# Three experts fixed ahead of the routing, the third one's weights in the out product's buffers, and a sorted tile turned early

## What is computed

```python
scores = jax.nn.sigmoid((h @ router_w).astype(jnp.float32))
sel = scores + router_b.astype(jnp.float32)
grouped = sel.reshape(T, N_EXPERT_GROUPS, EXPERTS_PER_GROUP)
gscore = lax.top_k(grouped, TOP_K)[0].sum(-1)
g = jnp.argmax(gscore, axis=-1)
in_group = jnp.take_along_axis(grouped, g[:, None, None], axis=1)[:, 0]
_, loc = lax.top_k(in_group, TOP_K)
expert = g[:, None] * EXPERTS_PER_GROUP + loc
...
hg = jnp.einsum('td,edf->tef', h, w_gate)
hu = jnp.einsum('td,edf->tef', h, w_up)
act = jax.nn.silu(hg) * hu * gates[..., None].astype(h.dtype)
return jnp.einsum('tef,efd->td', act, w_down)
```

## Time and profile before

| | us |
|---|---|
| median of three runs | 548.09 (547.16 to 549.73) |
| span of the profiled execution | 544.1 |
| TensorE busy (matmul) | 480.4, 88% |
| VectorE busy | 236.0, 43% |
| ScalarE busy | 148.2, 27% |
| GpSimd busy | 104.4, 19% |
| moved by DMA | 164.64 MB, mean 303 GB/s |

### The profile page before, as it was taken

The page is one execution under the profiler, slowest core; times in us unless marked ns, Lnnn a source line. Parts: engine busy times, 40 slices in busy tenths (PEclk is TensorE's granted clock), DMA queues, the critical chain, the costliest instruction groups (busy, mean ns, idle before and its releaser), DMA issues. The chain is left out here.

```text
span 544.1 us, 8978 instructions
## 1 busy us (share of the span) xinstructions
PE 480.4 (88%) x3278; PEld 233.3 (43%) x3279; DVE 236.0 (43%) x590; ACT 148.2 (27%) x289; POOL 104.4 (19%) x187
## 2 busy tenths in 40 slices
PE   2788979899969999995996999899998999999893
PEld 1135669655559644573344333333333333333331
DVE  2698994999963300867663101111011101111045
ACT  3645794532147610151102010110001100101142
POOL 3000250988870203500500000000000000000300
PEclk9988999999999999995998999999999999999998
DMA  8993046449497999220696999999999999999932
GB/s 278 339 400 112 1 154 217 166 166 363 143 391 269 369 366 417 82 86 1 239 385 243 410 423 418 418 418 416 421 421 419 419 417 419 417 420 421 403 120 116
DMA packets 42571, 164.64 MB, mean 303 GB/s; under 512 B 3314, under 2 KB 4106, under 8 KB 32676
## 3 DMA queue, kind: packets, MB, share of 16 engines
q1 hardware_dynamic: 35440, 144.22, 67.3%
q10 hardware_dynamic: 4580, 11.91, 5.8%
q0 software_dynamic: 2512, 7.99, 4.0%
HBM read 152.77 MB, written 11.34 MB: 302 GB/s over the span
## 5 line engine op out<-in xcount | busy, mean ns | idle before, releaser
L754 PE MATMUL psum<-arena 128*64 128x512 f32 x672 | 150.7, 601 | 16.7 <-DVE arena L1656 7.8
L754 PEld LDWEIGHTS psum<-arena 128*64 128x64 f32 x672 | 49.8, 138 | 103.7 <-issue 101.9
L767 PE MATMUL psum<-arena 128*64 128x512 f32 x336 | 75.9, 592 | 0.0
L1661 DVE TENSOR_TENSOR arena<-arena,psum 128x256 f32<-128x256 f32 x21 | 8.8, 421 | 143.4 <-ACT arena L1110 143.2
L1916 POOL DMA_INDIRECT arena<-sorted_outputs,src_u x6 | 5.7, 951 | 244.1 <-DMA sorted_outputs<-arena 242.6
L767 PEld LDWEIGHTS psum<-arena 128*64 128x64 f32 x336 | 25.7, 137 | 45.9 <-issue 45.9
L1110 ACT ACTIVATE arena<-psum 128x256 f32<-128x256 f32 x21 | 8.0, 383 | 130.0 <-PE psum L754 114.5
L664 PE MATMUL psum<-arena 128*128 128x512 f32 x96 | 42.2, 594 | 0.0
L1125 ACT ACTIVATE arena<-psum 128x512 f32<-128x512 f32 x19 | 11.3, 597 | 58.0 <-PE psum L767 58.0
L664 PEld LDWEIGHTS psum<-arena 128*128 128x128 f32 x96 | 17.9, 190 | 21.2 <-issue 20.9
L1656 DVE COPY arena<-arena 128x512 f32 x31 | 13.1, 423 | 30.4 <-issue 30.4
(11 more groups left out here) (355 smaller groups left out, 657.3 us busy)
## 6 DMA issues: line engine op xcount, KB each, us to landing
arena<-in_w_gate SPq DMA_DIRECT2D x32, 1024.0 KB, 15.7
arena<-in_w_up SPq DMA_DIRECT2D x32, 1024.0 KB, 18.1
arena<-in_w_down SPq DMA_DIRECT2D x16, 2048.0 KB, 15.2
arena<-in_w_mod SPq DMA_DIRECT2D x12, 2048.0 KB, 13.0
arena<-in_w_in SPq DMA_DIRECT2D x3, 2048.0 KB, 19.2
sorted_outputs<-arena ACTq DMA_DIRECT2D x38, 128.0 KB, 6.3
arena<-in_w_out SPq DMA_DIRECT2D x2, 2048.0 KB, 16.7
arena<-modulation_rows ACTq DMA_DIRECT2D x4, 1024.0 KB, 10.7
```

Of the source, the lines that this page charges most:

```text
L754: last = mm(bank[0][HALF * t:HALF * t + HALF, :], xs[:, side, k, :], gu[:, :, k, t * 256:t * 256 + 256], start=(k == 0), stop=(k == KD - 1))
L767: last = mm(bank[4][HALF * h:HALF * h + HALF, :], hiddenT[:, s * P + t * HALF:s * P + t * HALF + HALF], dn[:, 2 * t + s, h * 512:h * 512 + ...
```

## The change

Experts 0, 4 and 8 (`EARLY`) now stand at places 0, 1 and 2 whatever the counts. Set 2 has gate and up in slots 7 and 8 and down in slot 6, and the third's gate and up are issued as soon as the out product has ended. The sorted tiles move to slot 6 (tiles 0 to 3; tile 3 lies over the routing tiles, tile 4 over the picked first rows), and tile 5 takes tile 0's place, once that has been turned. TensorE turns tile 0 right behind the second gate product of expert 0, ahead of its down product. SP asks for the fourth's gate and up ahead of the third's down. When expert 0 has at most 128 rows, its unneeded passes are counted in `gated` before tile 0 is turned. The second key has changed: by rank, the turn is rank + 1.75 up to rank 9 and half the rank from rank 10, which puts the smallest experts between the largest.

```diff
+EARLY = (0, 4, 8)
...
-        hsr = view(slot(7), 6, D)
+        hsr = [view(at, D) for at in (slot(6), slot(6) + 1024, slot(6) + 2048, slot(6) + 3072, F + 12544, slot(6))]
...
-            b = (3, 0, 6)[j]
-            return view(slot(b), 2, KD, DE), view(slot(b + 2), 4, D)
+            gu, dn = ((3, 5), (0, 2), (7, 6))[j]
+            return view(slot(gu), 2, KD, DE), view(slot(dn), 4, D)
...
-            load_down(1, 1)
+            load_down(1, EARLY[1])
+            sp.wait_ge(S("wo_ready"), 6)
+            load_gate_up(2, EARLY[2])
+
+            def load_sorted(t):
+                sp.dma_start(hsr[t], hsd[t * P:(t + 1) * P, :]).then_inc(S(f"hs_in{t}"), 16)
+
             sp.wait_ge(S("tok_sent"), 16 * 6)
-            for t in range(6):
-                sp.dma_start(hsr[:, t, :], hsd[t * P:(t + 1) * P, :]).then_inc(S(f"hs_in{t}"), 16)
-            sp.wait_ge(S("first_ready"), 1)
+            sp.wait_ge(S("pad_sent"), 48)
+            sp.wait_ge(S("first_ready"), 4)
+            for t in (0, 1, 2):
+                load_sorted(t)
+            load_sorted(4)
             sp.wait_ge(S("onehots_done"), 1)
-            sp.wait_ge(S("pad_sent"), 48)
             sp.wait_ge(S("int_done"), 1)
-            third = expert_at(2)
-            for k, sem in ((0, "gu_in2"), (KD // 2, "gu_rest2")):
-                sp.dma_start(expert_weights(2)[0][:, 0:1, k:k + KD // 2],
-                             wg[:, bass.ds(third, 1), k:k + KD // 2, :]).then_inc(S(sem), 16)
+            load_sorted(3)
+            fourth = expert_at(SETS)
+            sp.wait_ge(S("hs_ready"), 2)
+            load_sorted(5)
+            sp.wait_ge(S("gated"), PASSES)
+            load_gate_up(0, fourth)
             sp.wait_ge(S("hs_ready"), 12)
-            for k, sem in ((0, "gu_in2"), (KD // 2, "gu_rest2")):
-                sp.dma_start(expert_weights(2)[0][:, 1:2, k:k + KD // 2],
-                             wu[:, bass.ds(third, 1), k:k + KD // 2, :]).then_inc(S(sem), 16)
-            load_down(2, third)
-            for e in range(SETS, NE):
+            load_down(2, EARLY[2])
+            sp.wait_ge(S("downed"), PASSES + 1)
+            load_down(0, fourth)
+            for e in range(SETS + 1, NE):
                 reload(e % SETS, e)
...
             with pe.If(first_n > HALF):
-                second_pass(0, 0, 0)
-            for t in range(6):
+                gate_up(0, turn(1, 0), None, 1)
+                with pe.If(first_n > P):
+                    sorted_columns(0)
+                    down(0, 1, turn(1, 0), turn(0, 0))
+                    transposes(turn(1, 0))
+                with pe.Else():
+                    pe.wait_ge(S("gated"), turn(2, 0))
+                    pe.sem_inc(S("gated"), PASSES - 2)
+                    sorted_columns(0)
+                    down(0, 1, turn(1, 0), turn(0, 0))
+                    transposes(turn(1, 0))
+                    pe.wait_ge(S("crossed"), turn(2, 0))
+                    pe.wait_ge(S("downed"), turn(2, 0))
+                    pe.sem_inc(S("crossed"), PASSES - 2)
+                    pe.sem_inc(S("downed"), PASSES - 2)
+            with pe.Else():
+                skipped(0, 1)
+                sorted_columns(0)
+            for t in range(1, 6):
                 sorted_columns(t)
...
-            d(V_.memset(prio[:, 0:1], 65536.0))
-            d(V_.memset(prio[:, 1:2], 32768.0))
             dve.wait_ge(S("tri_done"), 1)
-            d(cp(prio[:, 2:NE], desc[:, 2:NE]))
+            for i, e in enumerate(EARLY):
+                d(V_.memset(prio[:, e:e + 1], 65536.0 / 2 ** i))
+                d(cp(prio[:, e + 1:(*EARLY, NE)[i + 1]], desc[:, e + 1:(*EARLY, NE)[i + 1]]))
...
-            v(ts(turn_key, rank, 0.15, None, ALU.mult))
-            for r in (2.0, 4.0):
-                v(stt(turn_key, rank, r, turn_key, ALU.is_equal, ALU.add))
+            v(ts(counted_rank, rank, 0.5, 1.75, ALU.mult, ALU.add))
+            v(stt(counted_rank, rank, 9.5, counted_rank, ALU.is_lt, ALU.mult))
+            v(stt(turn_key, rank, 0.5, counted_rank, ALU.mult, ALU.add))
```

More of the change, by code:

```diff
@@ L409, in _ @@
             sp.wait_ge(S("fin_done"), 1)
-            load_gate_up(0, 0)
-            load_down(0, 0)
+            load_gate_up(0, EARLY[0])
+            load_down(0, EARLY[0])
             sp.wait_ge(S("unit_used"), 15)
-            load_gate_up(1, 1)
+            load_gate_up(1, EARLY[1])
             sp.wait_ge(S("yt_done"), 4)
             sp.wait_ge(S("modd_in5"), 32)
-            load_down(1, 1)
-            sp.wait_ge(S("tok_sent"), 16 * 6)
-            for t in range(6):
-                sp.dma_start(hsr[:, t, :], hsd[t * P:(t + 1) * P, :]).then_inc(S(f"hs_in{t}"), 16)
-            sp.wait_ge(S("first_ready"), 1)
+            load_down(1, EARLY[1])
[3 more added lines that the diff above has]
+                sp.dma_start(hsr[t], hsd[t * P:(t + 1) * P, :]).then_inc(S(f"hs_in{t}"), 16)
+            sp.wait_ge(S("tok_sent"), 16 * 6)
+            sp.wait_ge(S("pad_sent"), 48)
[3 more added lines that the diff above has]
+            load_sorted(4)
             sp.wait_ge(S("onehots_done"), 1)
-            sp.wait_ge(S("pad_sent"), 48)
             sp.wait_ge(S("int_done"), 1)
-            third = expert_at(2)
-            for k, sem in ((0, "gu_in2"), (KD // 2, "gu_rest2")):
-                sp.dma_start(expert_weights(2)[0][:, 0:1, k:k + KD // 2],
-                             wg[:, bass.ds(third, 1), k:k + KD // 2, :]).then_inc(S(sem), 16)
-            sp.wait_ge(S("hs_ready"), 12)
-            for k, sem in ((0, "gu_in2"), (KD // 2, "gu_rest2")):
-                sp.dma_start(expert_weights(2)[0][:, 1:2, k:k + KD // 2],
-                             wu[:, bass.ds(third, 1), k:k + KD // 2, :]).then_inc(S(sem), 16)
-            load_down(2, third)
-            for e in range(SETS, NE):
+            load_sorted(3)
[4 more added lines that the diff above has]
+            load_gate_up(0, fourth)
+            sp.wait_ge(S("hs_ready"), 12)
+            load_down(2, EARLY[2])
+            sp.wait_ge(S("downed"), PASSES + 1)
+            load_down(0, fourth)
+            for e in range(SETS + 1, NE):
                 reload(e % SETS, e)
@@ L738, in sorted_columns @@
                         last = tr(bank[SORT_BANK[t][h]][:, kk * P:(kk + 1) * P],
-                                  hsr[:, t, :].rearrange("p (q k) -> p k q", k=KD)[:, k, :], ident[:, :])
+                                  hsr[t].rearrange("p (q k) -> p k q", k=KD)[:, k, :], ident[:, :])
                     last.then_inc(S("hs_ready"), 1)
@@ L847, in _ @@
             pe.wait_ge(S("hs_copied_v"), 6)
[L848 to L851, removed]
+            with pe.If(first_n > P):
+                gate_up(0, turn(2, 0), None)
+                down(0, 1, turn(2, 0), turn(1, 0))
+                transposes(turn(2, 0))
+                with pe.If(first_n > P + HALF):
+                    with pe.Fori(3, PASSES) as q:
+                        gate_up(0, q + turn(0, 0), None)
+                        down(0, 1, q + turn(0, 0), q + turn(0, 0) + -1)
+                        transposes(q + turn(0, 0))
+                with pe.Else():
+                    skipped(0, 3)
             with pe.Fori(0, 5) as i:
@@ L1618, in _ @@
             v(tt(larger, key.unsqueeze(1).broadcast_to(square), key.unsqueeze(2).broadcast_to(square), ALU.is_gt))
-            rank, turn_key = r1[:, 0, :], key
+            rank, turn_key, counted_rank = r1[:, 0, :], key, r2[:, 0, :]
             v(V_.tensor_reduce(rank, larger, AX.X, ALU.add))
-            v(ts(turn_key, rank, 0.15, None, ALU.mult))
-            for r in (2.0, 4.0):
-                v(stt(turn_key, rank, r, turn_key, ALU.is_equal, ALU.add))
+            v(ts(counted_rank, rank, 0.5, 1.75, ALU.mult, ALU.add))
+            v(stt(counted_rank, rank, 9.5, counted_rank, ALU.is_lt, ALU.mult))
+            v(stt(turn_key, rank, 0.5, counted_rank, ALU.mult, ALU.add))
             v(tt(larger, turn_key.unsqueeze(1).broadcast_to(square), turn_key.unsqueeze(2).broadcast_to(square), ALU.is_lt))
```

## The result

| | before | after |
|---|---|---|
| median | 547.62 us (four runs, 546.14 to 549.73) | 558.94 us (four runs, 556.82 to 563.32) |
| ratio | | 1.024, interval 1.020 to 1.028 |
| span of the profiled execution | 544.1 | 561.6 |

The prediction had 552.4, with 547.8 to 555.2 as its range. The direction holds, the size doesn't: 11.3 us by the medians (13.1 by the ratio) where 4.3 were expected. The profiled execution of after is the slowest of its four (563.32); the spans of the other three are 555.1, 555.1 and 559.3.

The account below looks back on a forecast made before the run. PE sets the pace from 293.58, with the weight stream arriving just in time. Span 544.1 + 1.6 (early tile) + 2.7 (last place's wait) = 548.4; runs' median 4.0 above the profiled span gives 552.4 us, range 547.8 to 555.2.

Parts of the forecast that it names:

- The order of the places: Turn order: the three-pass expert moves from place 7 to place 3, delaying place 6's gate and up request to 351.2.
- the dry spell: Weight stream ahead of place 6's request: 7 to 9 us with nothing to move, just before 352.
- the last place as the one that pays: Last gate product: its wait on up weights becomes 3.5 where it was 0.8, +2.7 us (+1.9 to +3.7).
- The early tile: PE's queue between expert 0's second gate product and down product: 0.97 + 0.6 = 1.6 us later (1.0 to 1.9).
- The early load of the third: After the out product at 237: the third's gate and up (4.19 MB) land by about 250, at no cost.
- Nothing changes behind the last down product: End of the kernel: from the last down product to the end nothing should change.
- Rival 1: Weight stream: early loads carry over, no wait on the last place, only the front's shift stays; 548.9, chance 0.21.
- 364.7 + 145.1: Last place's second half lands at 509.8: place 6's landing plus 145.1 us of unbroken stream as before.
- The same bytes follow in the new order: Stream from place 6 to the last place: same bytes as before, no later request after its predecessor has landed; 145.1 us.
- the edits that cost nothing: Key arithmetic, early third load, new waits ahead of sorted loads, and earlier tile 5 and fourth's loads: no cost.
- The fourth's gate and up go at about 282 in place of 292: SP's queue behind tile 0's transposes: the fourth's request goes out earlier, listed as costing nothing.
- K: Theory from the experiments, not the prediction: TensorE's long branch comes at unneeded-pass jumps; which one depends on places jumping in a row.

Follow-up runs that it names:

- e10: As e8, with the turn key made so that all sixteen experts stand as in the kernel before; 545.84 us, ratio 1.001.
- e2: The changed kernel with the old form of the turn key, three-pass expert at place 8; 550.52 us, ratio 1.010.
- e3: The kernel before with the new keys alone: experts 0, 4, 8 first and the new turn order; 557.67 us, ratio 1.021.
- e6: The changed kernel's buffers, SP order and experts 0, 4, 8, with the old key form and TensorE's program of before; 550.41 us, ratio 1.009.
- e5: As e2, without the never-entered block of expert 0's third and later passes; 549.28 us, ratio 1.007.
- e1: The changed kernel, with the fourth's gate and up asked for only when place 1's rows are staged; 553.48 us, ratio 1.010.
- e7: As e5, with tile 0 turned behind expert 0's down product and last transposes, not ahead of them; 547.34 us, ratio 1.002.
- e4: The kernel before with an extra 2.1 MB HBM-to-HBM copy asked for when the third sorted tile has been turned; 551.32 us, one run.
- e8: As e6, but with experts 0, 1 and 3 fixed at the first places; 550.42 us, ratio 1.011.
- e9: The kernel before with experts 0, 1, 3 fixed and the new form of the turn key; 562.21 us, ratio 1.030.

## Why the prediction was wrong in size

**Right.** The order of the places, the dry spell and the last place as the one that pays: the request for place 6 32.75 behind place 3, about six us without transfers (7 to 9 predicted), place 6 there at 375.8 (363.9 in the prediction, 375.5 when moved by the 11.6 that place 2 is late). The early tile: 1.4 against 1.6. The early load of the third costs nothing (e10). Nothing changes behind the last down product. Rival 1, a head start that is kept, was rightly refused for this order; e10 has the third's head start under the old one, and even there it is worth nothing.

**Mis-sized: the last place, +2.7 predicted, +6.0 measured.** The term was the landing of the last piece at 364.7 + 145.1, where 364.7 is place 6's landing at 363.9 and 0.8 for a gap behind it. Moved by the 11.6 that place 2 is late, that landing should have been at 375.5 and was at 375.8, 0.3 late. From there to the last piece it took 148.8 (to 524.6), where 145.9 were charged. The step that failed is "The same bytes follow in the new order": 61.94 MB moved in that stretch at a mean of 416 GB/s, where before moved 60.78 at 419 in its 145.1 us. The 1.16 MB more are 2.8 us at 419 GB/s. The lower rate is the gap, about 1.0 where 0.8 was charged: place 6's down weights were asked for at 374.43, with its gate and up there at 375.8, too close to keep the engines fed (317 GB/s in 376 to 380). So 0.3, 0.2 and 2.8 are the difference between 2.7 and 6.0.

More than half of the bytes are found in the last place, which took 19.7 against 18.1: 8.25 MB against 7.58, all of the difference in ScalarE's queue (2.09 against 1.40). ScalarE asks there for the rows and weights of the last norm, 1.5 MB in two transfers. The second goes out at 515.27, 9.4 us ahead of the last piece's landing, in before at 503.59, only 3.4 ahead. By these times a late last piece is made later by transfers that it would otherwise have left behind it. The delay of the second half is 5.67 of waits (0.83 before) and 1.7 of lower clock (5.35 in place of 3.65) in the first half; the slow half isn't a cost of its own here, since a faster one would have waited 1.7 longer for the same landing.

By the figures of the Trainium skill (DMA: Bandwidth & Descriptors, Anatomy of one DMA), which are for the other descriptor path, a cold request of 4.19 MB would take 11.6 us, an estimate. It took 13.1 (362.72 to 375.8), so the trace decides against that estimate; the prediction's 12.7 is nearer.

**Missed: the jump, +4.4, for which the prediction had nothing.** It had place 1's gate product at 295.2 and the pause ahead of it as before. The step that failed is among the edits that cost nothing: "The fourth's gate and up go at about 282 in place of 292", and with it that TensorE's new waits and branches were costed as waits and tiles alone. The trace of before has every branch of TensorE with its duration, the shortest 65 and the longest 442 ns, and nothing in it says that one could take six us. The runs show this of it (the fourth column is the start of the q8 packet, from the start of the jump; the fifth is the end of the jump, from the start of that packet):

| kernel | DMA share, GB/s during it | branch, us | to the q8 packet | from it to the end | what it cost |
|---|---|---|---|---|---|
| after | 1.01, 398 | 6.67 | 4.4 | 2.3 | 4.4 of pause |
| e2 | 1.01, 405 | 6.23 | 3.9 | 2.3 | 3.9 |
| e3 | 1.03, 425 | 5.98 | 3.5 | 2.5 | 4.0 |
| e6 | 1.01, 419 | 5.90 | 3.4 | 2.5 | 4.0 |
| e5 | 0.30, 41 | 3.84 | 1.5 | 2.4 | 1.9 |
| e1 | 0.04, 9 | 3.77 | 1.0 | 2.8 | 1.5 |
| e7 | 0.28, 41 | 3.35 | 1.0 | 2.4 | 1.4 |

Over the same jump, e1 against after, full DMA engines make it 2.9 longer. Of the cost, what would have been idle anyway is taken off (3.6 for staging ahead of place 1; 0.7 between other places). In all seven a q8 packet of kind "instruction" runs during the jump, and the jump ends 2.3 to 2.8 us behind that packet's start, whatever the traffic; what the traffic changes is when the packet comes, 1.0 to 1.5 us into the jump or 3.4 to 4.4. That says what is waited for; whose instructions a packet holds isn't recorded, so the link stays an inference, though a close one. The Trainium skill (Runtime: NRT & Kernel Launch, Instruction fetch mechanics) has it so: instructions are fetched ahead in blocks, in sequence and by DMA, and a taken branch out of the fetched window forces a fetch of its target before anything goes on. The trace agrees in kind, with the packets above; the page has no price. By it the question to ask of the change would have been which never-run blocks TensorE jumps over; what the DMA engines do meanwhile is what the runs add.

**What stays open.** Why before, e4, e8, e9 and e10 have no long jump at all although they jump over the same blocks. K fits before, e3, e4, e6, e8, e9 and e10 (two one-pass places at the head give one; one place doesn't), but not e5 and e7, where the jump is already long behind the first such place, nor after, e1 and e2, where it is the block of expert 0. In every kernel that has one there is exactly one, and it lies between 290.9 and 324.6. In before, q8 packets run at 295.0, 301.0, 307.6, 319.1, 328.6 and 341.9, which is while TensorE goes through its loop over the experts for the first time (places 1 to 3, to 340), and none between 342 and 521. That fits code that is fetched once, on the first way through, with one jump that comes ahead of its fetch; I haven't shown it, nor what decides which jump. A kernel with the never-run block moved to the end of the program would have told; it wasn't tried.

**The sum again.** 1.4 for the tile, 4.4 for the jump and 6.0 for the stream make 11.8, where the medians say 11.3 and the ratio 13.1. By the ratios, taking the order back (e2) gave 7.5 us for the 6.0, and taking the jump ahead of place 1 out on top of it (e5) 2.0, which is the 3.9 of e2 less the 1.9 of the new long jump. Each ratio is uncertain by two or three us, so these agreements within 1.5 us are as close as they can be read. Executions of one kernel differ by several us, among other things in whether and for how long a product behind a pause runs at the lower clock.

## What to carry to other kernels

With a stream of weights that only just keeps up, ask of each reordering where the items that hold a buffer long stand: one three-pass expert three places ahead of a request emptied the queue (e8 has the same, shorter, with two passes), and a head start given earlier is lost at the first empty queue (after against e3). A row of short ones at the end may outrun it (16 us of transfer against 11.5 of work each); no run shows that by itself. And a block that is never run isn't free: look in the trace for the longest branch, not only the median, and don't start a large transfer just ahead of a jump that turned out long. Where the last transfer of a stream comes late, look also at what was meant to follow it and now goes ahead of it.

## What the runs showed of the hardware

A compare-and-branch on TensorE's sequencer took 0.07 to 0.56 us in all twelve profiles, but for one in each of seven, which took 3.3 to 3.8 us with the DMA engines mostly idle (shares 0.04 to 0.30) and 5.9 to 6.7 us with them full. A packet of instructions ran in each, and the jump ended 2.3 to 2.8 us behind its start. The view of waits puts this under "issue", under PE's sequencer, or even under the staging copy that had long been done.

After a pause TensorE often ran its next product at a granted clock of about 0.7, so part of it at 1.2 GHz in place of 2.4: a gate product of 7.09 took 10.02 after 8.00 us of idle, 9.43 after 7.49, 9.65 after 4.67, 8.51 after 5.10; half a gate product of 3.65 took 5.35 after 3.81, 5.62 after 5.87 and 6.35 after 3.65 (e3). The cost doesn't follow the length of the pause: after 3.60 to 3.62 the gate product took 8.48 to 10.07 in nine kernels, as much as after 8.00. After 2.57 (e5), 2.08 (e7) and, for half a product, 3.01 (e4) it lost nothing. So each of these pauses of 3.6 and more cost 1.4 to 3.0 more than its own length, unless a wait on weights followed.
